# Splitting the first weight transfer of an encoder kernel and moving four parameter rows behind it

## The reference, cut to what matters

```python
h = rmsnorm(x, norm_mix)          # x / rms(x) * g
proj = h @ w_in                   # 1024 -> many columns; split into xa, ya, uv, z, xbc, dt, gates
xbc = silu(conv4(xbc, conv_c_w) + conv_c_b)
xa  = conv4(xa, conv_a_w) + conv_a_b
```

## Time and profile before

| | us |
|---|---|
| runs, median of 3 (lowest to highest) | 963.28 (962.44 to 967.35) |
| profiled execution, device time | 962.54 |
| its span | 960.8 |

### The profile page before, as it was taken

How to read it: one execution, slowest core, us unless ns; L and a number is a source line. 1 busy time by engine, 2 the same in 40 slices (tenths; PEclk the granted TensorE clock), 3 DMA queues, 4 the chain that set the end, 5 groups by cost and what they waited for, 6 DMA issues and landing times.

```text
span 960.8 us, 18449 instructions
## 1 busy us (share of the span) xinstructions
PE 815.9 (85%) x8065; PEld 643.9 (67%) x8065; DVE 340.8 (35%) x873; ACT 191.7 (20%) x357; POOL 324.5 (34%) x169
## 2 busy tenths in 40 slices
PE   9999999999999999999999996756657666667565
PEld 7999988889999999999887653323323333333232
DVE  4788323647264434244213452112112112121112
ACT  3342138731231000102012111011110111110102
POOL 5876630038998879996300000000000000000000
PEclk9999999999999999999999999889898899898998
DMA  9854534443564344456598999999999999999995
GB/s 315 253 176 177 184 124 161 146 146 118 176 220 167 130 158 162 176 176 238 216 432 339 403 426 426 428 426 428 430 430 426 428 430 430 426 430 430 427 426 225
DMA packets 62529, 284.98 MB, mean 297 GB/s; under 512 B 6709, under 2 KB 11657, under 8 KB 50313
## 3 DMA queue, kind: packets, MB, share of 16 engines
q1 hardware_dynamic: 58200, 280.84, 73.4%
q10 hardware_dynamic: 4272, 3.32, 1.2%
HBM read 283.08 MB, written 1.06 MB: 296 GB/s over the span
## 4 chain that ended last, share of the span: by engine, by line
PE 58%; DMA 36%; DVE 2%; ACT 2%; POOL 1%; issue 1%; SPq 0%; DVEq 0%; ACTq 0%; POOLq 0%
DMA ring<-in_w_down_dram 35%; PE bank L1739 32%; PE bank L1625 7%; PE bank L1734 5%; PE bank L2042 4%; PE bank L2013 2%; PE bank L1698 1%; PE bank L1979 1%; PE bank L1895 1%; PE bank L1875 1%; DMA ring<-in_w_in_dram 1%; PE bank L1813 0%; PE bank L1834 0%; PE bank L1800 0%; PE bank L1799 0%
## 5 line engine op out<-in xcount | busy, mean ns | idle before, releaser
L1739 PE MATMUL bank<-blk,ring 128*128 128x128 f32 x1840 | 213.6, 275 | 0.4 <-POOL blk L569 0.4
L1739 PEld LDWEIGHTS bank<-blk,ring 128*128 128x128 f32 x1840 | 209.4, 192 | 2.0 <-issue 1.8
L2013 PE MATMUL bank<-ring,cbm 128*32 128x256 f32 x1760 | 127.6, 439 | 79.0 <-DMA ring<-in_w_gate_up_dram 78.4
L2013 PEld LDWEIGHTS bank<-ring,cbm 128*32 128x32 f32 x1760 | 59.3, 122 | 136.0 <-DMA ring<-in_w_gate_up_dram 92.4
L2042 PE MATMUL bank<-ring,cbm 128*32 128x256 f32 x928 | 62.1, 412 | 45.8 <-DMA ring<-in_w_down_dram 43.8
L1465 DVE TENSOR_TENSOR cbm<-bank,gq 128x256 f32<-128x256 f32 x31 | 13.2, 424 | 243.6 <-PE bank L1979 243.6
L1625 PE MATMUL bank<-blk,ring 128*128 128x256 f32 x384 | 85.4, 381 | 0.8 <-DVE blk L1387 0.8
L533 POOL TENSOR_TENSOR ring<-ring 128x1024 f32<-128x1024 f32 x20 | 47.3, 2365 | 97.1 <-DVE dec L1185 75.6
L1625 PEld LDWEIGHTS bank<-blk,ring 128*128 128x128 f32 x384 | 72.2, 190 | 11.6 <-DVE blk L1387 1.2
L2042 PEld LDWEIGHTS bank<-ring,cbm 128*32 128x32 f32 x928 | 29.8, 116 | 74.5 <-DMA ring<-in_w_down_dram 53.5
L1739 PE MATMUL bank<-ring 128*128 128x128 f32 x608 | 71.0, 275 | 0.0
(11 more groups left out here) (351 smaller groups left out, 987.8 us busy)
## 6 DMA issues: line engine op xcount, KB each, us to landing
ring<-in_w_gate_up_dram SPq DMA_DIRECT2D x55, 2048.0 KB, 27.3
ring<-in_w_down_dram SPq DMA_DIRECT2D x28, 2048.0 KB, 27.3
ring<-in_w_in_dram SPq DMA_DIRECT2D x19, 2048.0 KB, 7.9
blk<-in_w_gate_up_dram SPq DMA_DIRECT2D x7, 2048.0 KB, 23.2
ring<-in_w_kv_dram SPq DMA_DIRECT2D x4, 2048.0 KB, 7.9
ring<-in_w_a_proj_dram SPq DMA_DIRECT2D x2, 2048.0 KB, 8.7
ring<-in_w_b_proj_dram SPq DMA_DIRECT2D x2, 2048.0 KB, 8.6
ring<-in_w_c_proj_dram SPq DMA_DIRECT2D x2, 2048.0 KB, 7.8
```

The lines of the kernel that those rows point to most:

```text
L1739: last = mm(out_[:, f], wt[:, k, f * P:(f + 1) * P], xt[:, k, :], start=k == 0, stop=k == 3)
L2013: last = mm(gu_bank(p)[c * WIN:(c + 1) * WIN, 0:2 * SEG], xe[:, xin, 4 * j + k, :], w[:, k, :, c, :], start=4 * j + k == 0, stop=4 * j + k ...
```

## The change: the diff

The first quarter of slab 0 is moved as two transfers of one k tile (256 KB each) instead of one of two k tiles (512 KB); the other three quarters stay. PE waits for the part that begins at the k tile. The four sets of convolution rows are issued by SP after the parts of slab 0 and no longer by ACT; `gmix` stays with ACT. `spread_rms` is called after k tile 1 instead of 0, without `to_par(0)`, which is called after k tile 5. The list `order` and the readers' waits are as before.

```diff
+        OPENING = ((0, 1), (1, 2), (2, 4), (4, 6), (6, 8))
...
-            for q in range(4):
-                sp.dma_start(ring[:, 0, q * 2 * 512:(q + 1) * 2 * 512].rearrange("p (k n) -> p k n", k=2),
-                             w[0].rearrange("(k p) n -> p k n", p=P)[:, 2 * q:2 * q + 2, c0:c0 + 512]
-                             ).then_inc(quarter[q], 16)
+            for i, (k0, k1) in enumerate(OPENING):
+                sp.dma_start(ring[:, 0, k0 * 512:k1 * 512].rearrange("p (k n) -> p k n", k=k1 - k0),
+                             w[0].rearrange("(k p) n -> p k n", p=P)[:, k0:k1, c0:c0 + 512]
+                             ).then_inc(first_part[i], 16)
+            for tile, row, ap, n in rows:
+                if tile == 0 and row > 0:
+                    sp.dma_start(prow[row:row + n, tile, :], ap).then_inc(sem["par0_loaded"], 16)
...
-                if tile == 0:
-                    act.dma_start(prow[row:row + n, tile, :], ap
-                                  ).then_inc(sem["gmix_loaded" if row == 0 else "par0_loaded"], 16)
+                if tile == 0 and row == 0:
+                    act.dma_start(prow[row:row + n, tile, :], ap).then_inc(sem["gmix_loaded"], 16)
...
             def spread_rms():
 
-                to_par(0)
                 pe.wait_ge(sem["diag_ready"], 1)
...
-                if k % 2 == 0:
-                    pe.wait_ge(quarter[k // 2], 16)
+                for i, (k0, _) in enumerate(OPENING):
+                    if k == k0:
+                        pe.wait_ge(first_part[i], 16)
...
-                if k == 0:
+                if k == 1:
                     spread_rms()
+                if k == 5:
+                    to_par(0)
```

More of the change, by code:

```diff
@@ L344, in encoder_kernel @@
                 for f in sorted({family(n) for n in order})}
-        quarter = [ctx.enter_context(nc.semaphore(f"first_slab_quarter{i}")) for i in range(4)]
+        OPENING = ((0, 1), (1, 2), (2, 4), (4, 6), (6, 8))
+        first_part = [ctx.enter_context(nc.semaphore(f"first_slab_part{i}")) for i in range(len(OPENING))]
         filled = [ctx.enter_context(nc.semaphore(f"slot_filled{i}")) for i in range(RING)]
```

## The result

The changed kernel takes 969.16 us (median of 7 runs, 968.30 to 970.86) against 963.43 (7 runs, 962.44 to 967.35): 5.73 us or 0.6% slower, ratio 1.0060 with a 95% interval from 1.0050 to 1.0069. Forecast were 968.6, in a range from 966.8 to 970.6, and 5.7 us of loss. Its profiled execution took 969.16 with a span of 967.1, 6.3 us more than before.

A forecast was written before the change was run, and what follows sets the result against it. PE's chain was taken to bound the opening, with the expert weight stream waiting on PE. A 5.3 us stall plus 0.4 of clock made 5.7 us slower: 968.6 us, set between 968.2 and 969.0, range 966.8 to 970.6.

The forecast's parts named there:

- The early start: PE's first weight product: the smaller first transfer lets it start at 7.0 instead of 8.05, 1.05 us won.
- The row copy: ACT's copy of the rms row: released by the parameter rows' transpose, the sixth finished unit, at 18.2 instead of 10.63.
- POOL's chain and the slack: Row copy to `hT`, combinations, weight sums: 7.6 us later, less 2.3 spare at product 3, so 5.3 us of stall.
- S1: POOL's weight sum of slab 1 that PE's product 1 waits for: ready at 28.7 instead of 21.11.
- second difference: POOL's second weight difference of slab 1, before PE's product 2: ready at 31.1 instead of 23.54.
- S2: POOL's weight sum of slab 1 that PE's product 3 waits for: ready at 33.5 instead of 25.86.
- S4: POOL's last weight sum of slab 1: ready at 35.9 instead of 28.28, still before PE's product 5 at 37.2.
- The clock: PE's product 1 after 4.4 us idle: slowed from 1.79 to 3.35 us, mostly covered, 0.4 left, bounds 0 and 1.56.
- SP's queue at no cost: Five more issues on SP put slab 1 at most 2.9 us later, covered by transfers in hand until 11.2: cost nothing.
- The rival on the other side: ACT's row copy is released by the row product at 11.1, so only the early start remains: 961.5 us; 6%.
- The sum: Whole kernel: 5.3 us of stall plus 0.4 of clock, 5.7 us slower; 968.2 or 969.0 by base, set at 968.6.

The follow-up runs named there:

- rows_on_sp: The kernel before with only the four sets of convolution rows moved from ACT's queue to SP's, behind the quarters; 967.89 us, ratio 1.0042.
- split_only: The kernel before with only the first quarter split into two transfers of one k tile; 962.83 us, ratio 0.9989.
- own_count: The changed kernel with ACT's row copy waiting for five finished units and DVE's copy of the parameter rows for six; 963.49 us, ratio 1.0000.
- late_turn: The kernel before with only the parameter rows turned after k tile 5 instead of in front of the row product; 971.35 us, ratio 1.0078.
- turn_after_k3: The changed kernel with the parameter rows turned after k tile 3 instead of 5; 965.69 us, ratio 1.0019.
- kept_busy: The changed kernel with 18 products of ones into an unused bank between products 0 and 1 of slab 1; 970.62 us, ratio 1.0075.
- slab1_between: own_count with slab 1 issued between the convolution rows and the rows of tile 1; 963.01 us, ratio 0.9995.
- slab1_first: own_count with slab 1 issued straight after the parts of slab 0, ahead of the parameter rows; 964.15 us, ratio 1.0005.

## Why the prediction was right

*The early start.* Forecast 7.0 with a gain of 1.05; measured 7.22 and 0.83. The k tile was not what PE waited for; its own transposes were. The list of DMA issues gives the us from issue, at 1.70, to landing of the first weights; before, rows_on_sp, split_only, changed:

```profile
ring<-in_w_in_dram SPq DMA_DIRECT2D x1, 512.0 KB, 6.3
ring<-in_w_in_dram SPq DMA_DIRECT2D x1, 512.0 KB, 5.9
ring<-in_w_in_dram SPq DMA_DIRECT2D x1, 256.0 KB, 5.6
ring<-in_w_in_dram SPq DMA_DIRECT2D x1, 256.0 KB, 5.0
```

The k tile landed at 6.7, in the forecast 6.6 to 7.1. Not all of this is the split: by these single executions the split alone brings the landing from 8.0 to 7.3, and moving the rows off ACT's queue alone brings it to 7.6. The prediction had counted the rows only as 0.06 MB among the bytes of the old quarter. The rule of the Trainium skill's page "DMA: Bandwidth & Descriptors", section "Anatomy of one DMA — SWDGE (gpsimd) path", a constant 2.0 us for each transfer, would have given 7.9, by the prediction's estimate. The starts at 6.95 to 7.28, without a wait for DMA, are against it for these transfers, which SP issues and not GpSimd, whose path the page describes.

*The row copy.* Forecast 18.2, measured 18.41; the difference is the start's. Released by L1654 as forecast. Of the steps this is the one that own_count, late_turn and turn_after_k3 show: taken away, done alone, and made smaller.

*POOL's chain and the slack.* S1, second difference, S2 and S4 forecast for 28.7, 31.1, 33.5 and 35.9, measured 28.88, 31.33, 33.64 and 36.07. No duration changed by more than 0.02 us. The price is the delay less the slack: 7.8 - 2.3 = 5.5 on the measured numbers, and with the clock 5.88. The 0.2 over the forecast 5.3 is the later start.

*The clock.* Forecast: it falls, product 1 takes 3.35, and 0.4 us are left (its own times give 33.9 - 33.6 = 0.3). Measured 3.60 and, against kept_busy, 5.88 - 5.30 less the earlier start, 0.36. What is covered depends on how long the lower level lasts; in late_turn 1.5 us were left.

*SP's queue at no cost.* Right for the changed kernel, but for a reason that the prediction did not give, and its price without the cover was read from the wrong user. It named 22.8, PE's first product, as the first use of slab 1. The first user is POOL's weight sum, at 18.76 before. There it landed at 18.7, with nothing to spare. Nor did the work in hand until 11.2 us make the later issue free: in own_count slab 1, issued at 9.49, before that bound, needed 11.8 us all the same, the engines moved 29 GB/s from 12 to 13 us, and POOL waited until 21.39. The issue 2.4 us later came through as a landing 2.6 us later. The cover was the late row copy, that is, the fault itself.

*The rival on the other side.* Its place held, and its point of decision, a row copy at about 12, agrees with slab1_between (11.21, no stall) and turn_after_k3 (15.26, a stall). Its price did not hold: for a row copy released by the row product 1.05 us less than the profiled execution before was forecast (961.5), and own_count, which is that kernel, gained nothing (963.49 against 963.67). The step that failed is the one above.

*The sum.* 5.7 us forecast, 5.73 measured between the medians. That they agree to 0.03 is luck: the interval of the ratio is about 4.8 to 6.6 us, the trace has 5.88 at 50 us, and 968.6 was set between two bases of which the higher, 969.0, was the nearer. The profiled spans differ by 6.3; the 0.45 us more than at the weight stream come in the expert stage, where slab1_between lost 0.8 and split_only too ended later than its start would have it. Differences of this size in the weight stream were not explained.

## What to carry to other kernels

Where readers count finished units on one semaphore, moving a unit that is off the path past one that is on it moves the release of the latter: list who waits for which number before moving anything. Price a delayed input by the tightest slack along the chain that it feeds, here 2.3 us at product 3 and not the 3.6 at product 1. And a cover that hides a cost may be the fault that one is about to mend: after the mending, look for the next wait, in the queue that the same change has reordered.

## What the runs showed of the hardware

- Small transfers issued behind a slab landed behind it: four sets of rows, 60 KB, issued by 6.0 us behind slab 0, landed at 12.5 (rows_on_sp). Behind slab 0 and slab 1 (slab1_first) the issues themselves were held up, one of them taking 3.14 us on SP, and PE's transpose, which waited for the rows, started at 20.01.
- Slab 1, 2 MB, issued by SP between 6.45 and 9.73 us, landed 11.0 to 12.1 us after its issue in eleven of the kernels (10.1 in rows_on_sp, 14.6 in slab1_first, where it was issued at 4.15). Issued later, it landed later by about as much, although slab 0 was still on its way.
- The lower clock after about the same idle of PE (4.17 us in both) cost about 0.4 us in the changed kernel and 1.5 in late_turn, by when the granted clock rose again: at about 32 us in the one, between 35 and 36 in the other. An idle of 2.83 us (rows_on_sp) was followed by a granted clock of 0.50 too, one of 1.47 us (turn_after_k3) by 1.00.
- PE's first eight transposes of x took 1.06 or 1.07 us in seven of the profiled executions and 1.18 to 1.94 in the others, with the same code and a granted clock given as 1.00. This moves the start by up to 0.9 us, as much as the early start won; the cause was not looked for.
